# A first stage of a two-block transformer kernel: fp32 weights multiplied as they land, filters and tables moved ahead, recurrence and heads re-timed

## The reference

```
mod = silu(c) @ ada_w + ada_b            # 2048 x 12288: sh1, sc1, g1, sh2, sc2, g2
h   = rms_norm(x) * norm1_g * (1 + sc1) + sh1
u, lru_gate, q, k, v, mix_gates = split(h @ w_in + b_in)
u   = causal conv over 4 tokens; r, i = sigmoid of 128x128 products per head
a   = exp(-8 r softplus(-lambda)); state = scan(a, sqrt(1 - a^2) * i * u)
y_lru  = state * gelu(lru_gate);  y_attn = windowed attention(q, k, v, sinks)
x  += g1 * ((sig(m1) * (y_lru @ w_lru_out) + sig(m2) * (y_attn @ w_attn_out)) @ w_o)
x  += g2 * ((silu(gate) * up) @ w_ffn_out);  x = rms_norm(x) * final_g
```

## Time and profile before

| | us |
|---|---|
| median of 3 runs | 2852.67 (2852.19 to 2854.4) |
| the profiled execution | 2859.61 |
| its span, first to last instruction | 2857.8 |
| TensorE busy | 2760.0 |
| VectorE busy | 1971.4 |
| ScalarE busy | 1405.1 |
| moved by DMA | 596.72 MB |

### The profile page before, as it was taken

How to read it: one execution, slowest core, us unless ns; L and a number is a source line. 1 busy time by engine, 2 the same in 40 slices (tenths; PEclk the granted TensorE clock), 3 DMA queues, 4 the chain that set the end, 5 groups by cost and what they waited for, 6 DMA issues and landing times.

```text
span 2857.8 us, 37594 instructions
## 1 busy us (share of the span) xinstructions
PE 2760.0 (97%) x14828; PEld 2362.7 (83%) x14828; DVE 1971.4 (69%) x2754; ACT 1405.1 (49%) x2079; POOL 13.7 (0%) x29
## 2 busy tenths in 40 slices
PE   6899999999999999999999999999989999999997
PEld 5687888888888788888888888887778888888886
DVE  6556888777788785555555567768567757766765
ACT  2235766664554454444434456554454434444443
POOL 0000000000000000000000000000000000000000
PEclk9889999999999999999999999999999999999999
DMA  9685577778888786655656566543546565555553
GB/s 331 212 297 161 159 257 240 243 259 309 284 282 296 237 278 190 192 190 182 190 190 190 185 187 190 192 147 120 173 151 200 190 192 181 192 190 182 191 192 126
DMA packets 161032, 596.72 MB, mean 209 GB/s; under 512 B 18087, under 2 KB 18120, under 8 KB 159512
## 3 DMA queue, kind: packets, MB, share of 16 engines
q1 hardware_dynamic: 158136, 575.11, 61.5%
q0 software_dynamic: 2720, 19.20, 1.9%
HBM read 590.05 MB, written 4.19 MB: 208 GB/s over the span
## 4 chain that ended last, share of the span: by engine, by line
PE 85%; DVE 8%; ACT 3%; issue 2%; DMA 2%; POOL 0%; SPq 0%; DVEq 0%; ACTq 0%
PE PS L624 84%; DVE WL L1649 2%; ACT WH L1108 1%; DVE ACC L1652 1%; DMA W<-in_ada 1%; DVE G L1649 1%; DMA W<-in_w_in 1%; DVE G L1652 1%; DVE G L1655 1%; PE PS L755 0%; DVE TT L1649 0%; ACT L1322 0%; ACT TT L1346 0%; DVE XBf L1649 0%; DVE XB L1649 0%
## 5 line engine op out<-in xcount | busy, mean ns | idle before, releaser
L624 PE MATMUL PS<-XA,WH 128*128 128x512 f32 (+1 forms) x4800 | 1660.1, 395 | 8.0 <-DVE WL L1649 4.8
L1649 DVE TENSOR_TENSOR WL<-W,WH 128x1024 fp32r<-128x1024 f32 x904 | 1099.0, 1223 | 626.9 <-ACT WH L1108 625.5
L624 PE MATMUL PS<-XA,WL 128*128 128x256 f32 x4608 | 1296.7, 281 | 0.0
L1108 ACT ACTIVATE WH<-W 128x1024 fp32r<-128x1024 f32 x904 | 947.6, 1055 | 544.8 <-PE PS L624 493.7
L624 PEld LDWEIGHTS PS<-XA,WH 128*128 128x128 f32 x4800 | 899.5, 191 | 219.2 <-issue 11.6
L624 PEld LDWEIGHTS PS<-XA,WL 128*128 128x128 f32 x4608 | 876.5, 190 | 2.8 <-issue 1.5
L624 PE MATMUL PS<-WH,XB 128*128 128x512 f32 x1440 | 446.5, 390 | 0.6 <-DVE G L1649 0.6
L624 PEld LDWEIGHTS PS<-WH,XB 128*128 128x128 f32 x1440 | 270.3, 188 | 57.1 <-DVE G L1649 0.9
L624 PE MATMUL PS<-WL,XB 128*128 128x512 f32 x720 | 280.2, 389 | 0.0
L1150 ACT ACTIVATE EV<-PS 128x256 f32<-128x256 f32 x248 | 94.5, 383 | 310.1 <-PE PS L624 305.7
L1652 DVE SCALAR_TENSOR_TENSOR ACC<-W,SM,ACC 128x1024 f32<-128x1024 f32 x164 | 209.7, 1279 | 7.7 <-DMA W<-in_ada 6.4
(11 more groups left out here) (209 smaller groups left out, 1462.2 us busy)
## 6 DMA issues: line engine op xcount, KB each, us to landing
W<-in_w_in SPq DMA_DIRECT2D x224, 512.0 KB, 5.0
W<-in_ada SPq DMA_DIRECT2D x192, 512.0 KB, 5.5
W<-in_w_ffn_in SPq DMA_DIRECT2D x176, 512.0 KB, 4.4
W<-in_w_up SPq DMA_DIRECT2D x176, 512.0 KB, 4.5
W<-in_w_ffn_out SPq DMA_DIRECT2D x88, 512.0 KB, 4.3
W<-in_w_down SPq DMA_DIRECT2D x88, 512.0 KB, 4.4
W<-in_w_lru_out SPq DMA_DIRECT2D x32, 512.0 KB, 5.4
W<-in_w_attn_out SPq DMA_DIRECT2D x32, 512.0 KB, 5.8
```

What stands on the lines that cost most here:

```text
L624: return e.matmul(o, l, r, start=start, stop=stop, skip_group_check=True)
L1108: return e.activation(o, a, ACT.Copy)
L1649: return e.tensor_tensor(o, a, b, op)
```

## The change

- PLAN: NU goes from 12 to 10, so 20 units stand in the first stage, 5 behind each of slabs 1 to 3 and 5 at the end; START is 84. WHOLE = 15 units are those of the first 12 k tiles.
- Units below WHOLE are multiplied as fp32 straight from W by xt_, which h_made has turned into h in place; no WH and WL for them. SP waits for TensorE (mm["unit", u]) before it fills their slot again. VectorE makes the low part of h for later gemms behind TensorE (h_low); ScalarE copies the high part.
- ADA_PE holds 4 half tiles of slab 0 only; the other 60 of slabs 0 to 3 are VectorE's.
- x is scaled on ScalarE. The sine layers are straight code ahead of the loops, the four window steps fall in slab 0 and use the four gemm banks (early), the kf products in slab 1.
- x, w3, window, ident and dft are issued by SP; POOL begins with the store of kf, behind entry 83.
- The ada half tiles behind START follow ADA_PACE.
- CONV starts at 1 instead of 6, the square of each quarter goes from VectorE to ScalarE, later steps of a quarter come one step sooner; the transposes of v come one gemm later; each head has one more step.

```diff
-ADA_PE = (3, 7, 11, 15)
-
-NU = 12
-UNITS_AFTER = (3, 5, 8, 10, 13, 15)
+
+ADA_PE = (2, 5, 8, 11)
+
+
+NU = 10
+UNITS_AFTER = (6, 8, 10, 12, 15)
+WHOLE = 12 * NU // 8
 
 
 PV = {}
...
+ADA_PACE = ((72, 112, 150, 176, 208, 240, 272, 325), (0, 10, 28, 52, 79, 97, 108, 129))
...
-        while ada and n >= 64 + 1.86 * (128 - len(ada)):
+        while ada and np.interp(n, *ADA_PACE) > 128 - len(ada):
...
-CONV = [6 + 5 * h // 2 for h in range(16)]
-LAST = [CONV[4 * q + 3] + 3 for q in range(4)]
+
+CONV = [1 + 5 * h // 2 for h in range(16)]
+GATED = [c + 3 for c in CONV]
+LAST = [GATED[4 * q + 3] for q in range(4)]
...
+        e.dma_start(zT, d["zT"]).then_inc(*loaded["z"]("zT"))
+        e.dma_start(w1, d["filt_w1_2"]).then_inc(*loaded["z"]("w1"))
+        e.dma_start(w2, d["filt_w2_2"]).then_inc(*loaded["z"]("w2"))
+        e.dma_start(RES[:, :, :], d["x"]).then_inc(*loaded["x"]("x"))
+        e.dma_start(w3, d["filt_w3_2"]).then_inc(*loaded["w3"]("w3"))
         for n, kind in enumerate(PLAN):
             if n >= RING:
                 m = n - RING
-                if m in UNIT_OF:
+                if m not in UNIT_OF:
+                    w.wait_ge(*(ape if m in ON_PE else adv)[m])
+                elif UNIT_OF[m] < WHOLE:
+                    w.wait_ge(*mm["unit", UNIT_OF[m]])
+                else:
                     w.wait_ge(*lo[UNIT_OF[m]])
-                elif m in ON_PE:
-                    w.wait_ge(*ape[m])
-                else:
-                    w.wait_ge(*adv[m])
             src = (d["ada"][kind[1], kind[2]] if kind[0] == "ada" else d[kind[0]][kind[1]])
             e.dma_start(W[:, n % RING, :], src[:, kind[-1] * 1024:(kind[-1] + 1) * 1024]).then_inc(*landed[n % RING](n))
             if n == RING - 1:
-                e.dma_start(zT, d["zT"]).then_inc(*loaded["z"]("zT"))
-                e.dma_start(w1, d["filt_w1_2"]).then_inc(*loaded["z"]("w1"))
-                e.dma_start(w2, d["filt_w2_2"]).then_inc(*loaded["z"]("w2"))
-
-    ON_PE = {n for n, k in enumerate(PLAN) if k[0] == "ada" and k[1] < 4 and 2 * k[2] + k[3] in ADA_PE}
+                e.dma_start(win, d["window"]).then_inc(*loaded["win"]("win"))
+                e.dma_start(IDN[:, :], d["ident"]).then_inc(*loaded["id"]("id"))
+                e.dma_start(CS, d["dft"]).then_inc(*loaded["cs"]("cs"))
...
-        e.dma_start(RES[:, :, :], d["x"]).then_inc(*loaded["x"]("x"))
-        e.dma_start(IDN[:, :], d["ident"]).then_inc(*loaded["id"]("id"))
-        w.wait_ge(*landed[12 % RING][12])
-        e.dma_start(w3, d["filt_w3_2"]).then_inc(*loaded["w3"]("w3"))
-        e.dma_start(win, d["window"]).then_inc(*loaded["win"]("win"))
-        e.dma_start(CS, d["dft"]).then_inc(*loaded["cs"]("cs"))
-        w.wait_ge(*landed[ADA_END[3] % RING][ADA_END[3]])
+        w.wait_ge(*landed[(START - 1) % RING][START - 1])
         w.wait_ge(*sl["kf", 7])
...
-                key = ("u", o)
-                b = bank_of(key)[:, o % 2 * S:(o % 2 + 1) * S]
-                w.wait_ge(*xl["h", kt])
+                b, begins, ends = bank_of(("u", o))[:, o % 2 * S:(o % 2 + 1) * S], t < NU and o % 2 == 0, kt == KT - 1
                 whi, wlo, names = columns(P)
-                mul(b, whi, XA[kt][:, 0:S], kt == 0 and o % 2 == 0, False)
-                mul(b, whi, XA[kt][:, S:2 * S], False, False)
-                m = mul(b, wlo, XA[kt][:, 0:S], False, kt == KT - 1)
-                names += [key] if kt == KT - 1 else []
+                if u < WHOLE:
+                    w.wait_ge(*hx[kt])
+                    m = mul(b, whi, xt_[kt], begins, False)
+                else:
+                    w.wait_ge(*xl["h", kt])
+                    mul(b, whi, XA[kt][:, 0:S], False, False)
+                    mul(b, whi, XA[kt][:, S:2 * S], False, False)
+                    m = mul(b, wlo, XA[kt][:, 0:S], False, ends)
+                names += [("u", o)] if ends else [("h", kt)] if o == NU - 1 else []
                 if names:
                     m.then_inc(*mm(*names))
...
         flt, xt = filters(), x_turns()
-        for n in range(START + 2):
+        layer(0, w1, zT)
+        layer(1, w2, fs[:, 1, :])
+        for n in range(START + 1):
             if n in ON_PE:
                 ada(n)
             if n in SLAB_ENDS:
@@ -812,18 +829,20 @@
             if n in X_STEPS:
                 next(xt)
             if n in FILTER_STEPS:
-                next(flt, None)
-            if n - 2 in UNIT_OF:
-                first_tiles(UNIT_OF[n - 2])
+                next(flt)
+            if n - 1 in UNIT_OF:
+                if n - 1 == ENTRY[0]:
+                    w.wait_ge(*fv["b", 3])
+                first_tiles(UNIT_OF[n - 1])
...
-            yield
-            yield
-            yield
+            for _ in range(4):
+                yield
...
+            w.wait_ge(*iv["x"])
+            w.wait_ge(*sqr["x", 1, 0])
+            for n in range(2):
+                for tb in range(2):
+                    c = slice(1024 * n, 1024 * (n + 1))
+                    e.activation(XS[:, tb, c], RES[:, tb, c], ACT.Copy, scale=inverse_of("x", tb)).then_inc(
+                        *xs(("x", n, tb)))
...
-        def h_high(q):
+        def h_made(q):
+
             w.wait_ge(*sv["sc1", q])
             for i in range(4 * q, 4 * q + 4):
                 w.wait_ge(*cp["x", i // 2])
                 c = 8 * q + i % 4
-                e.activation(XA[i][:, 0:S], xt_[i], ACT.Identity, scale=SC[:, i:i + 1],
-                             bias=MOD[:, c:c + 1]).then_inc(*xh(("h", i)))
-
+                if q < 3:
+                    e.activation(xt_[i], xt_[i], ACT.Identity, scale=SC[:, i:i + 1],
+                                 bias=MOD[:, c:c + 1]).then_inc(*hx(i))
+                else:
+                    e.activation(XA[i][:, 0:S], xt_[i], ACT.Identity, scale=SC[:, i:i + 1],
+                                 bias=MOD[:, c:c + 1]).then_inc(*xh(("h", i)))
+            if q < 3:
+                w.wait_ge(*hx[4 * q + 3])
+                for i in range(4 * q, 4 * q + 4):
+                    copy(XA[i][:, 0:S], xt_[i]).then_inc(*xh(("h", i)))
...
-                    if t == LAST[q] + 2:
+                    if t == LAST[q] + 3:
                         for j in range(4):
                             h, c = 4 * q + j, slice(j * S, (j + 1) * S)
                             i = e.activation(A4[:, c], R4[:, c], ACT.Exp, scale=SN[:, h:h + 1])
                         i.then_inc(*lra(("exp", q)))
-                    if t == LAST[q] + 5:
+                        w.wait_ge(*lra["exp", q])
+                        e.activation(R4, A4, ACT.Square).then_inc(*lra(("square", q)))
+                    if t == LAST[q] + 4:
                         w.wait_ge(*lrv["t4", q])
                         e.activation(T4, T4, ACT.Sqrt).then_inc(*lra(("sqrt", q)))
```

More of the change, by code:

```diff
@@ L297 @@
     ADA_SUM.setdefault(max(UNIT_OF[i] for i in range(ADA_END[_s]) if i in UNIT_OF) + 1, []).append(_s)
-ADA_LAST = {k[1]: i for i, k in enumerate(PLAN) if k[0] == "ada" and not (k[1] < 4 and 2 * k[2] + k[3] in ADA_PE)}
+ADA_LAST = {k[1]: i for i, k in enumerate(PLAN) if k[0] == "ada" and not (k[1] == 0 and 2 * k[2] + k[3] in ADA_PE)}
 ADA_OLD = {2: 0, 3: 1, 6: 2, 7: 3, 8: 6, 9: 7, 4: 8, 5: 9, 10: 4, 11: 5}
@@ L1660, in entry @@
                 s = u % USLOTS
+                if u < WHOLE:
+                    return
                 w.wait_ge(*hi[u])
@@ L1782, in chain, with filter_arg @@
             w.wait_ge(*sv.last())
+        def filter_arg(i):
+            k = 2 * i
+            freq, bias = (PVT[0:64, PV["filt"] + x:PV["filt"] + x + 1] for x in (k, k + 1))
+            w.wait_ge(*loaded["pv"]["pv"])
+            w.wait_ge(*flp["layer", i])
+            arg, t1 = fs[:, 0, :], fs[:, 2, :]
+            ts(arg, BANK["layer", i][0:64, 0:S], bias, freq, ALU.add, ALU.mult).then_inc(*fv(("layer", i)))
+            mg = 12582912.0
+            w.wait_ge(*fv.last())
+            ts(t1, arg, 1.0 / (2 * np.pi), mg, ALU.mult, ALU.add).then_inc(*fv())
+            w.wait_ge(*fv.last())
+            ts(t1, t1, -mg, None, ALU.add).then_inc(*fv())
+            c1 = 6.28125
+            c2 = round((2 * np.pi - c1) * 2.0**21) / 2.0**21
+            c3 = float(2 * np.pi - c1 - c2)
+            for c in (c1, c2, c3):
+                w.wait_ge(*fv.last())
+                stt(arg, t1, -c, arg, ALU.mult, ALU.add).then_inc(*fv())
+            w.wait_ge(*fv.last())
+            ts(arg, arg, 3.1415925, -3.1415925, ALU.min, ALU.max).then_inc(*fv(("arg", i)))
+        filter_arg(0)
         w.wait_ge(*sl["exp"])
```

193 lines of the change are left out of this document (87 added, 106 removed).

## The result

The changed kernel takes **2836.36 us** (median of 4 runs, 2835.41 to 2838.55) where the kernel before, on the same chip, takes 2853.53 (4 runs, 2852.19 to 2855.45): ratio 0.994, 95% interval 0.9923 to 0.9958. That is 17.2 us less, faster as forecast and inside the range, but a little less than half of the 35.5 us that I had summed. Between the two profiled executions it is 22.6 us of span (2857.8 to 2835.2). Executions of one kernel differ: the profiled one of before was 6.9 us above its median (that of the change 0.6), so all of my sum was made on a rather long one.

The account below looks back on a forecast made before the run. TensorE, busy 97% of 2857.8 us, was taken as the bound, leaving the start and single later waits. Gains of 24.5 and 13 less 2 lost make 35.5 us; taken from the median 2852.67 that gives 2817, range 2795 to 2841.

Parts of the forecast that it names:

- Start: Part before gemm ("u", 12): that gemm starts at 184.0 instead of 208.5 us, gain 24.5, bounds 10 to 48.
- slabs 2 and 3: In the start: ring transfers, landings and units in line make each slab last 32.5 us, done at 151.
- Slab 0: First ring entries, 0 to 15: VectorE begins near 17 us; the sum starts at 46 and ends at 50.
- Slab 1: In the start: six kf steps ahead of the first unit, which begins near 65 us; slab done at 86.
- Slab 2: Chain of sum, units and landings of 5.0 us: 30.1 at full clock, 35.3 partly at half; 32.5 taken.
- S: End of the last slab's sum in the start: 154 us instead of 184.3, with 30 more to ("u", 12).
- slabs of 38 ... gain 10 to 12: Lower bound for the start: slabs as long as the old kernel's last one, sum ending at 165 to 166.
- Rival C: Start: TensorE rests for landings around every unit, clock stays at 1.2 GHz; slower, 2874 us; chance 0.05.
- Later waits: Recurrence, v transposes and heads: two thirds of 19.2 us of waits and lost clock go, gain 13, bounds 6 to 19.
- Rival B: Start gains 24.5 or less, recurrence's waits change place, VectorE feeds WL late: 2828 to 2841 us; chance 0.16.
- ada pace: Units 150 to 208: more ada halves per unit load VectorE to 97%; 2 us lost, bounds 0 to 7.
- Rival A: Transfers alone bound the start, slots return fast: start gains 38 to 48, time 2786 to 2798 us; chance 0.12.

Follow-up runs that it names:

- experiment 2: The changed kernel with WHOLE = 0, no fp32 units, every first unit split by ScalarE and VectorE: 2831.1 us, ratio 0.9924 to the kernel before.
- experiment 6: The changed kernel with convolutions, square on VectorE, turns of v and head steps as in the kernel before: 2836.9 us, ratio 0.9946 to the kernel before.
- experiment 8: The changed kernel with recurrence, turns of v, head steps and ada spreading as in the kernel before, only its start kept: 2840.6 us, ratio 0.9958.
- Experiment 7: The changed kernel with the old rule spreading the ada halves (from n = 64, one per 1.86 units): 2842.9 us, ratio 0.9959 to the kernel before.
- experiment 10: The changed kernel with no fp32 units (WHOLE = 0) and each slab's units issued two or three ada halves earlier: 2829.4 us, ratio 0.9910.
- experiment 11: The changed kernel with no fp32 units, units issued earlier and each gate's product one step later (GATED = c + 4): 2824.3 us, ratio 0.9898.

## Why the prediction was right in direction and wrong in size

The saving fell short by 18.3 us (17.2 against 35.5). The start has 14.0 of it. The part behind ("u", 12) gave 12.1 between the traces (2648.9 to 2636.8) where 13 - 2 was forecast. The remaining 5.4 are the difference between the profiled pair (22.6) and the medians (17.2), which no row places.

**Start, forecast 24.5, measured 10.5.** This is the step that failed, in its part "slabs 2 and 3": I took 32.5 us a slab, and they measured 38.2 and 36.2. By terms:

- Slab 0: sum at 50.3 instead of 46, 4.3 late. Entry 0 of the ring lands at 14.95 instead of "near 12", but VectorE's sines end later still, and it begins its first entry at 16.40, forecast 17. From there to the sum it is busy 26.1 us and idle 7.8, where I had allowed 2. Its waits from 14 to 54 us, for halves of ada_w, TensorE's filter products, the window table and ScalarE's root (NS):

```profile
DVE ACC L1695 <- DMA W<-in_ada: 3.0, 3, 2.3
DVE G L1692 <- PE PS L634: 2.0, 3, 0.9
DVE G L1692 <- DMA XAf<-in_window: 1.3, 1, 1.3
DVE NS L1802 <- ACT NS L1195: 1.0, 1, 1.0
```

- Slab 1: 37.3 us from sum to sum instead of 40, so at 87.6 it was only 1.6 late. First unit at 67.3 (forecast 65), six kf steps ahead of it: as followed.
- Slab 2: the chain of the ring was the right one, its links were mis-sized: I took it at nearly full clock, though my own sum with the units behind the sum cold was 35.3, and a landing at 5.0. To the start of unit 5 I had 1.84 + 3.45 + 1.2 + 5.0 = 11.5; measured 104.31 - 87.62 = 16.7. The sum took 3.4 (91.06 - 87.62), unit 4 5.3, the issue went out at 97.22, 0.9 behind it, and the landing took 7.1 instead of 5.0. Then unit 5 took 5.3 (104.31 to 109.65) instead of 3.45, and the rest of the slab 16.2 instead of 15.2: 38.2 in all, 8.1 over the full clock's 30.1, of which my 32.5 had allowed 2.4. Half clock has 1.6 + 1.9 + 1.9 of the 8.1, the landing 2.1.
- Slab 3: 36.2, by the same pattern (125.82 to 142.14 is 16.3 us).
- S was 165.1 instead of 154, and from S to ("u", 12) 33.3 instead of 30: unit 14 and what follows ran at a mean clock of 0.94, (1 - 0.94) x 33.3 = 2.0, and 0.8 idle.

The landing of 5.0 was the median of the whole kernel. Here a slot comes free when the ring has drained, so the transfers go out in a burst, and the unit's is the third of it. The issues of the changed kernel at that place, and the median landings of those made from 95 to 100 us:

```profile
96.38 0.80 SPq L583 DMA_DIRECT2D W<-in_ada  x2
97.22 0.43 SPq L583 DMA_DIRECT2D W<-in_w_in  x1
97.70 1.50 SPq L583 DMA_DIRECT2D W<-in_ada  x2
...
W<-in_ada SPq DMA_DIRECT2D x4, 512.0 KB, 7.0
W<-in_w_in SPq DMA_DIRECT2D x2, 512.0 KB, 7.9
```

The bound I gave for this term, "slabs of 38 ... gain 10 to 12", is what happened; I had it from the trace of before and set it aside. (Its S of 165 to 166 with my 30 behind it gives 13, not 10 to 12; the 33.3 that was measured there makes it 10.5.) Rival C named the mechanism, units that rest for a landing and run cold, and was right for the units around the slabs' ends (5.29, 5.50, 5.39 us) and wrong for the rest, which ran at 3.6 to 3.7.

Of the Trainium skill's two rules that I weighed, the burst that starts cold behind each DMA wait (TensorE: Matmul & The Clock Gate, HAM oscillation) agrees with the trace for the units at 104.31 and 142.14, behind waits of 7.96 and 9.12 us. It doesn't cover the cold unit at 127.63, behind 1.79 us of waiting for VectorE, and units behind landings waited for 1.30, 1.12 and 0.85 us (at 120.31, 152.07 and 156.64) ran warm, at 3.72. The 358 GB/s (HBM Reference, Specifications) decided nothing, and I had misread it: the same section gives it for two cores that stream together, and about 425 for a core alone, with which the 412 of the kernel before and the 378 of experiment 2's slab 3 agree.

**What the start's gain consists of** is known in part, each figure from one undoing and with some 6 us of scatter on it: ada off TensorE gives 9 (207.6 against 198.4), the fp32 products cost 8 (198.4 against 190.0). I had credited the fp32 products' side, VectorE's relief and the slots. The tables' placement of the kernel before, NU, the order of the units, the scaling of x and the filters moved ahead were not undone one by one, so what they give or cost is open.

**Later waits, forecast 13, measured 12.5 in the profiled pair, but not for the reason given.** The named checks held: no wait at the turns of v, none at the heads, 1.2 us for WL. Rival B's sentence held too, that the recurrence's waits change place: 7.0 us for the gates. The edits themselves are worth 0.5 to 3.1 us by medians (experiments 6 and 8), not clear of the spread, and at most 2.5 + 3.4 = 5.9 by the trace's idle and half clock. I took two thirds of 19.2; it was 6 at most. The start alone already has 8.1 of the 12.1 us behind ("u", 12) (2840.2 - 199.4 = 2640.8). Whether part of the 19.2 belonged only to the one long execution that I read, a second profile of the kernel before would have to show.

**ada pace, forecast 2 lost.** Experiment 7 shows 0.2 between the traces: nothing lost. VectorE was busy 136.5 of 160 us from 560 to 720 and TensorE never rested there.

**Chances.** The time, 2836.4, is that of rival B (2828 to 2841), to which I had given 0.16, and it lies in my range only because the range takes B in. In B the start gains less than 24.5 and the waits change place, which is what occurred. But B has nothing won behind the start and WL late; the traces have 12.1 won and 1.2 us of waits for WL, so that its number fits is in part luck. Rival A needed the slots back fast; the runs that come nearest, experiments 10 and 11, give 187, not 161 to 170, with the DMA engines at 0.95 in slabs 2 and 3 of experiment 10.

What stays open: why the median of "pace as before" is 6.5 us higher when its trace shows 2 of it, how much of the 6.6 us in experiment 8 is scatter, and where the 5.4 us between the profiled pair and the medians lie.
